# A new table of how many expert slots each stage of a fused encoder step takes, and an earlier call for TensorE's late adds

## What is computed

```python
h = rms_norm(x); proj = h @ w_in
y_r = rwkv7_group(proj[..., :P_RWKV])      # 8 heads x 64, delta-rule recurrence with a state
y_a = swa_group(q, k, v)                   # 8 q heads, 2 kv heads, window of 2 chunks, sink logit
x = x + concat(y_r, y_a) @ w_out
# PEER: product keys, 128 x 128 experts, 8 heads x 16 experts for each token
q = (t @ w_q).reshape(T, 8, 2, 128)        # t = rms_norm(x)
v1, i1 = top_k(q[:, :, 0] @ key1.T, 16);  v2, i2 = top_k(q[:, :, 1] @ key2.T, 16)
best_s, pos = top_k(v1 (+) v2, 16);  expert = (i1 * 128 + i2)[pos];  gate = softmax(best_s)
act = gelu(einsum('thed,td->the', down[expert], t))
x = x + einsum('the,thed->td', gate * act, up[expert])
y = rms_norm_final(x)
```

## Time and profile before

| | |
|---|---|
| median of three runs | 4259.82 us (4251.76, 4259.82, 4260.77) |
| the profiled execution | 4251.79 us, its span 4250.0 us |
| mean granted TensorE clock | 0.864 |
| busy: PE, DVE, POOL, ACT | 77%, 68%, 34%, 33% |
| moved by DMA | 1413.08 MB, 332 GB/s on the mean; the expert rows 1208.03 MB of it |

### The profile page before, as it was taken

How to read it: one execution, slowest core, us unless ns; L and a number is a source line. 1 busy time by engine, 2 the same in 40 slices (tenths; PEclk the granted TensorE clock), 3 DMA queues, 4 the chain that set the end, 5 groups by cost and what they waited for, 6 DMA issues and landing times.

```text
span 4250.0 us, 44182 instructions
## 1 busy us (share of the span) xinstructions
PE 3255.1 (77%) x14236; PEld 1821.3 (43%) x14236; DVE 2905.9 (68%) x5934; ACT 1418.3 (33%) x4074; POOL 1435.1 (34%) x1158
## 2 busy tenths in 40 slices
PE   9996836887787787869786877788778868786656
PEld 5554533452545253526352544354344525452222
DVE  1003355759776977697679767876887597769765
ACT  1001102433352435233523352344244323523323
POOL 0000002424343344334333433343344243424554
PEclk9997667998889888979887989798989988898879
DMA  4102227999899899989997999799989997999998
GB/s 190 52 38 82 86 74 289 398 401 375 316 401 409 322 367 413 409 319 375 413 390 312 389 406 391 313 391 412 385 334 399 397 379 315 399 381 362 422 422 370
DMA packets 223286, 1413.08 MB, mean 332 GB/s; under 512 B 25619, under 2 KB 34323, under 8 KB 72134
## 3 DMA queue, kind: packets, MB, share of 16 engines
q0 software_dynamic: 165888, 1208.03, 70.4%
q1 hardware_dynamic: 55878, 190.35, 11.7%
q10 hardware_dynamic: 1296, 11.94, 0.7%
HBM read 1391.06 MB, written 20.41 MB: 332 GB/s over the span
## 4 chain that ended last, share of the span: by engine, by line
DVE 32%; PE 26%; DMA 14%; ACT 6%; issue 5%; POOL 1%; another core or an unknown queue 0%; DVEq 0%; SPq 0%; POOLq 0%; PEldq 0%; ACTq 0%
DVE ex_rows L1495 14%; PE mx_ps L1469 10%; DMA ex_rows<-experts,ex_expert_c 9%; PE mx_ps L1213 4%; DVE ex_x2c L1505 2%; DMA mx_fac<-w_q 2%; DMA mx_ex<-w_out 2%; DVE mx_pqb L1313 2%; DVE mx_fac L1314 2%; PE mx_ps L996 1%; DVE mx_pqb L1311 1%; PE mx_ps L1003 1%; PE mx_ps L960 1%; ACT ex_diag L1451 1%; PE mx_ps L1196 1%
## 5 line engine op out<-in xcount | busy, mean ns | idle before, releaser
L1432 POOL DMA_INDIRECT ex_rows<-experts,ex_expert_c x1152 | 1433.8, 1245 | 2781.9 <-PE mx_ps L1469 1283.6
L1469 PE MATMUL mx_ps<-ex_rows,ex_diag 128*128 128x512 f32 x3096 | 1650.8, 679 | 365.0 <-ACT ex_diag L1451 353.2
L1495 DVE CUSTOM_DVE_ANT_0 ex_rows<-ex_rows,ex_tnc 128x1024 f32<-128x1024 f32 x1152 | 1375.5, 1222 | 222.4 <-DMA ex_rows<-experts,ex_expert_c 206.5
L1469 PEld LDWEIGHTS mx_ps<-ex_rows,ex_diag 128*128 128x128 f32 x3096 | 628.2, 215 | 1227.8 <-issue 1223.3
L1441 ACT ACTIVATE ex_coef<-ex_coef 128x1 f32<-128x1 f32 x1152 | 222.9, 202 | 1549.4 <-DVE ex_coef L1495 1533.8
L1505 DVE SCALAR_TENSOR_TENSOR ex_x2c<-ex_rows,ex_coef,ex_x2c 128x1024 f32<-128x1024 f32 x378 | 485.3, 1284 | 136.5 <-ACT ex_coef L1444 129.4
L1444 ACT ACTIVATE ex_coef<-ex_coef,ex_gate_c 128x1 f32<-128x1 f32 x1152 | 283.7, 285 | 9.7
L1451 ACT ACTIVATE ex_diag<-cn_ident,ex_coef 128x128 f32<-128x128 f32 x774 | 283.3, 392 | 9.3
L260 PE MATMUL psP<-pj_w_in_sb,pj_hT 128*128 128x432 f32 x768 | 279.6, 526 | 0.0
L229 DVE TENSOR_SCALAR pj_proj_sb<-psP,pj_rstd_a 128x432 f32<-128x432 f32 x27 | 18.0, 668 | 277.7 <-PE psP L260 243.7
L260 PEld LDWEIGHTS psP<-pj_w_in_sb,pj_hT 128*128 128x128 f32 x768 | 145.4, 190 | 130.1 <-issue 130.1
(11 more groups left out here) (293 smaller groups left out, 3945.5 us busy)
## 6 DMA issues: line engine op xcount, KB each, us to landing
mx_fac<-w_q SPq DMA_DIRECT2D x54, 512.0 KB
mx_ex<-w_out SPq DMA_DIRECT2D x36, 512.0 KB
mx_ex<-w_q SPq DMA_DIRECT2D x36, 512.0 KB
ex_rows<-experts,ex_expert_c POOLq DMA_INDIRECT x1152
mx_p_cur<-w_q SPq DMA_DIRECT2D x27, 512.0 KB
mx_xs<-w_q SPq DMA_DIRECT2D x27, 512.0 KB
proj_rows<-pj_proj_sb ACTq DMA_DIRECT2D x9, 1296.0 KB, 4.7
mx_p_cur<-proj_rows SPq DMA_DIRECT2D x9, 1296.0 KB, 8.7
```

The lines of the kernel that those rows point to most:

```text
L1432: pool.indirect_dma_start(rows[:, g % RING, :], None, A["experts"], bass.IndirectOffsetOnAxis(expert_c[:, s:s + 1], 0))\
L1469: last = pe.matmul(bank(6 + c), diag[:, n % DIAGS, :], up[:, r, c * 512:(c + 1) * 512], start=n == 0, stop=n == len(ON_PE) - 1)
L1495: dve.tensor_tensor_reduce(out=down[:, r, :], in0=down[:, r, :], in1=tnc[:, :], scale=1.0, scalar=0.0, op0=ALU.mult, op1=ALU.add, accum_ou ...
```

## The change

`STAGES` gets eleven entries in place of fifteen, with other numbers of slots and other shares, and `mix_tensor` gets one call `slots.upto(5)` ahead of its wait for the sigmoids. The ring of 11 rows and the lags of one and two marks stay as they are. The number of slots that DVE adds is 42 by the new table too.

```diff
 BEGIN, END = 6, MARKS + 4
-STAGES = ((6, 2, 0.5), (7, 4, 0.5),
-          (16, 19, 0.4),
-          (25, 16, 0.4),
-          (28, 7, 0.2),
-          (38, 21, 0.3),
-          (42, 5, 0.7),
-          (48, 9, 0.8),
-          (59, 17, 0.0),
-          (67, 13, 0.0),
-          (71, 4, 0.3),
-          (MARKS + 1, 1, 0.5), (MARKS + 2, 0, 0.5), (MARKS + 3, 5, 0.5), (END, 5, 0.5))
+STAGES = ((7, 3, 0.3),
+          (16, 21, 0.5),
+          (25, 18, 0.4),
+          (28, 7, 0.1),
+          (38, 22, 0.3),
+          (42, 7, 0.7),
+          (48, 11, 0.8),
+          (59, 16, 0.0),
+          (67, 12, 0.0),
+          (71, 2, 0.3),
+          (END, 9, 0.3))
 ADD_LAG, PE_LAG = 1, 2
@@ mix_tensor
             last.then_inc(lora_out.sem, 1)
+            slots.upto(5)
             pe.wait_ge(sig_ready.sem, sig_ready.due(t, 1))
             pe.matmul(bank(4), rc[:, TRI_X:TRI_X + P], sa[:, 0, :], start=True, stop=True)
```

## The result

The changed kernel takes 4316.48 us (median; 4305.98 to 4323.04) where the kernel before, run beside it, takes 4255.79: a ratio of 1.0137, 95% interval 1.0119 to 1.0155. It is slower, as forecast, but by some 60 us and not 20; it lies outside the range.

The account below looks back on a forecast made before the run. No engine was full; DVE, TensorE or DMA bounded each stretch of a turn. A turn: -3.5 + 1 + 0 + 5 = +2.5 us; eight turns +20 on 4251.79, plus 8.0 to the median: 4280 us, range 4232 to 4312.

Parts of the forecast that it names:

- Direction: Whole kernel: slower, 0.57; same 0.18; faster 0.25; forecast 4280 us.
- the weights behind a loaded row queue: Router's projections, marks 43 to 48: rows issued earlier share DMA engines and delay weight blocks; +5 us a turn.
- the early rows of the forecast: Marks 43 to 48: rows 83 to 86 out by about 3337, 87 to 91 by about 3359; five rows more, 12.5 us of traffic.
- The turn's end: Marks 60 to 77: two dots and one add less on DVE's chain, TensorE's late adds offset the rest; -3.5 us (-5 to +1).
- The four late adds: Turn's end, ahead of the sums: four TensorE adds let in by the new call, taken as 9 us.
- Marks 6 to 38: Scan and attention: 3 to 4 us won early, lost to the train of landing rows; +1 us (-1 to +4.4).
- Marks 39 to 42: Start of the router's projections: DVE's two more dots and an add, 3.5 us, fit its 9.47 us gap; 0.
- Marks 43 to 48: Router's projections: a row queue loaded until about 3385 delays the weights TensorE needs; +5 us a turn (0 to +8).
- The alternative count by bytes: Marks 43 to 48: only two of five rows are extra traffic, 5 us less 3.5 to spare; +1.5 us.
- The last tile: Last tile runs one slot a mark; its last slot goes from DVE to TensorE, under 1 us once; 0.

Follow-up runs that it names:

- E14: Changed kernel with entry (48, 11, 0.8) split so that the dots of slots 81 and 83 come one mark later; 4254.5 us, ratio 1.0014.
- E4: Changed kernel loading only half the columns of each weight block (256 KB, rows of 2 KB), matmuls on stale halves; 4188.89 us in one execution.
- E5: Changed kernel with its 24 weight blocks loaded as twelve pairs in rows of 8 KB, same bytes, half the packets; 4230.95 us, ratio 0.9943.
- E7: Changed kernel with each weight block loaded by two DMAs of half its columns, rows of 2 KB, twice the packets; 4331.62 us, ratio 1.0182.
- E9: Changed kernel with weight blocks 15, 17, 19, 21 and 23 issued from ScalarE instead of SyncE, a second weight queue; 4261.8 us, ratio 1.0012.
- E11: Changed kernel with 9 and 18 slots in marks 43 to 48 and 49 to 59 in place of 11 and 16; 4239.62 us, ratio 0.9958.
- E6: Kernel before with its weights loaded as twelve pairs of blocks in rows of 8 KB; 4299.25 us, ratio 1.0108.
- E10: Kernel before with weight blocks 15, 17, 19, 21 and 23 issued from ScalarE, a second weight queue; 4297.12 us, ratio 1.0088.
- E3: Changed kernel with 5, 9 and 20 slots in marks 39 to 42, 43 to 48 and 49 to 59, not 7, 11, 16; 4280.73 us, ratio 1.0061.
- E13: Changed kernel with 7, 7 and 20 slots in marks 39 to 42, 43 to 48 and 49 to 59, not 7, 11, 16; 4240.84 us, ratio 0.9966.
- E8: Changed kernel with weight pairs in 8 KB rows and 5, 9 and 20 slots in marks 39 to 59, not 7, 11, 16; 4298.99 us, ratio 1.0095.
- E12: Changed kernel with 7, 8 and 19 slots in marks 39 to 42, 43 to 48 and 49 to 59, not 7, 11, 16; 4236.42 us, ratio 0.9949.

## Why the prediction was right or wrong

**Direction: right, and in part by luck.** The sign came from the term that carries it, the weights behind a loaded row queue, and that term is what the traces show. But its size as forecast would not have been enough. E14 has the early rows of the forecast and issues the later ones only behind the weights, and its turn is 1.2 us longer than before, 1.0014 in time: hardly a change. What made the kernel clearly slower are rows that the forecast did not have.

**The turn's end: the steps right, the size short.** -3.5 was forecast; measured are -5.6 to L1515 and another -1.1 from L1223 to the hand-over, where marks 60 to 67 have one dot less. The turn handed over at the first line; kernel after.

```profile
3554.02 0.20 DVE L1478 COPY ex_expert_c<-mx_expert 128x64 uint32<-128x64 uint32 x1
3577.98 0.17 DVE L762 TENSOR_SCALAR mx_small<-mx_small 128x8 f32<-128x8 f32 x1 [1.53 <-ACT mx_small L670]
...
3587.01 1.27 DVE L1506 SCALAR_TENSOR_TENSOR ex_x2c<-ex_rows,ex_coef,ex_x2c 128x1024 f32<-128x1024 f32 x1
3595.47 0.69 DVE L776 SCALAR_TENSOR_TENSOR mx_fac<-mx_pqb,mx_ex 128x512 f32<-128x512 f32 x1 [7.18 <-ACT mx_ex L675]
```

```profile
3573.04 0.36 ACT L665 ACTIVATE mx_loraT<-mx_ps 128x256 f32<-128x256 f32 x1
...
3581.72 1.02 ACT L672 ACTIVATE mx_sa<-mx_ps 128x1024 f32<-128x1024 f32 x1 [2.47 <-PE mx_ps L936]
```

```profile
3581.62 9.82 PE L1470 MATMUL mx_ps<-ex_rows,ex_diag 128*128 128x512 f32 x16
3591.27 1.02 PE L941 MATMUL mx_ps<-mx_sa,cn_rc 128*128 128x512 f32 x2
```

L762 stands 3.2 us sooner behind the hand-over. The four late adds take 9.82 us (9 forecast), the sums start 9.55 us behind L672 (8), DVE idles 7.18 us ahead of L776 (6). The forecast's times are those of the turn before, in which mark 73 begins at 3498.6, 16.6 us behind the hand-over; here it begins at 3568.23, 14.2 behind it, so they are to be read from there. L665 comes 4.8 us behind that point (5.1 forecast), L672 13.5 (14.3), L768 14.6 (15.3) and L776 27.2 (28.3). In this turn L1515 is 3.1 us sooner, with the 1.1 about what was forecast.

The rest of the size is TensorE's clock. This turn is one of three of the seven in which it is at its lower level for all four products L935/L936. In the other four L672 comes 1.7 to 2.5 us sooner, and L1515 stands 37.7 to 42.7 us behind the hand-over where it is 44.2 to 44.5 in the three. The earliest of them, handed over at 1892.0:

```profile
1914.70 1.12 PE L936 MATMUL mx_ps<-cn_g2b,mx_loraT 1*128 1x512 f32 x2
1915.75 7.13 PE L1470 MATMUL mx_ps<-ex_rows,ex_diag 128*128 128x512 f32 x16
```

Its granted clock is 1.00 from 1912 to 1922.8, the upper level, and the turn lasts 411.4 us where the three have 417.2 to 418.9. In the kernel before L776 stands at 44.9 to 45.2 in every turn. The forecast took the lower level for the products in each turn; so the -6.7 in all lie outside its range of -5 to +1. What raises the clock in one turn and not in another stays open.

In the turn at 3554.02 GpSimd's hole is 10.08 us (18.64 in the earlier trace rows), and the engines move 184 GB/s from 3575 to 3590 (36 in the earlier trace rows).

```profile
3586.21 0.97 POOL L1433 DMA_INDIRECT ex_rows<-experts,ex_expert_c  x1 [10.08 <-PE mx_ps L1470]
```

**Marks 6 to 38: right within 2 us.** From L1515 to L884 2.9 us are won (3 to 4 forecast): 5.6 by L819, of which 2.7 are lost again. By L1196 2.2 more are taken back, so the whole is -0.7 us, where I took +1 from a range of -1 to +4.4. The landing rows set the time, as forecast: DVE waits 15.7 us in ten waits from 3727 to 3779, where it waited 12.5 in nine.

```profile
DVE ex_rows L1496 <- DMA ex_rows<-experts,ex_expert_c: 15.7, 10, 2.5
```

**Marks 39 to 42: right within a microsecond**, 0 forecast, +0.9 measured.

**Marks 43 to 48: the step that failed.** The forecast had +5 us (0 to +8), the runs +14.9. Its mechanism is right: queues taken in turn by packets (E4, E5, E7, E9), rows 87 to 91 early. Without the four later rows (E11 to E14) the stretch is 44.6 to 45.3 us, so by difference these five cost about 8, the upper end of the range; no run moves them alone. What it lacks is rows 92 to 95. The text lets the row queue run dry "about 3385", by the rows that it listed, and looked only at adds "ahead of any wait for the router's results". But slot 81's add, which stands behind such waits, had moved too, from mark 49 to mark 46 (its dot from mark 47 to 44), ahead of the ninth query block; it frees four more rows before the queue is empty, and these cost the other 6.5 us (E14, which takes them away, has 45.3 for 51.8). The mistake of method: I counted what was early at the start of the stretch and priced it with the length of the old stretch, instead of going on, add by add, until the last block had landed. The alternative count by bytes, +1.5, is refuted: 8 us for five rows and 6.5 for four are 1.6 us a row, less than the 2.5 in which one lands but far more than the forecast's remainder of 1.5 for all.

**The last tile: 0 forecast, wrong in two places that nearly cancel.** The tail is 12.0 us shorter, turn 1 7.8 us longer than the other turns' loss. The new table has 117 slots due by mark 67, the old 113: four more must be done before the hand-over in the first turn, and four fewer remain behind the last one, at 2.5 us a row. All thirteen traces with the new shape of the table (117 slots by mark 67) have 343.8 to 347.8 us behind the last hand-over, the four with the old one 357.6 to 358.6. My sentence looked at the last tile's own slots, not at those left over from the tile before.

## What to carry to other kernels

When DMA queues share the engines, count packets in each queue over a window first: if the counts are equal, the smaller packets lose, and a load can be sped up by larger rows or by a second queue, at a price of its own (6 us a turn here in the kernel that did not need it, E6 and E10). Then compare schedules again: here the new table lost by 61 us with the weights as they were, and won by 68 us with pairs and by 35 with two queues. What a transfer that starts sooner costs is not its bytes but how long it keeps its queue loaded ahead of a load that someone waits for; follow each release, add by add, until the last such load has landed. With work spread over marks, ask which release changes sides of a wait: here two dots moved by one mark were worth 52 to 62 us, while two, three or four slots fewer in the stage gave one and the same stretch.

## What was unexpected

The loss has a ceiling. Doubling the weights' packets (E7) made a block take 6.3 us in place of 3.76 and the turn only 1.6 us longer, as the rows behind ran out. And a low clock of TensorE can be free: 0.64 of full for 8 us in E3 against 1.00 in E13, with no difference at the end of the stretch, as PE waited for weights there; at the turn's end, where others wait for PE, it was worth up to 7 us a turn. Left open: what sets the clock there, 1.8 of the 8 us a turn by which E8 is slower than E5, and the 0.9 us of marks 39 to 42. Fastest of all was E5 (4230.95 us), then E12 (4236.42, from another run beside its own kernel before); the two together were not tried.
